# One decoder trunk on one core: the delta rule's recurrence moved into the next head's levels, its projection regrouped

## The reference, cut to what matters

```python
def chunk_gated_delta_rule(q, k, v, g, beta):          # 8 heads, chunks of C tokens
    gc = cumsum(g); decay = exp(gc_i - gc_j) for i >= j, else 0
    a_mat = strict lower part of (k*beta) k^T * decay
    t_mat = inverse of (I + a_mat)                       # triangular solve
    u = t_mat @ (v * beta);  w = t_mat @ (k * beta * exp(gc))
    qk = lower part of q k^T * decay
    for each chunk:                                      # lax.scan: the recurrence
        v_new = u - w @ state
        o     = (q * exp(gc)) @ state + qk @ v_new
        state = state * exp(g_last) + (k * exp(g_last - gc))^T @ v_new

def mixer_c(h, ...):                                     # layer 2 of 4
    qkv, gate, b, a = split(h @ w_in)                    # then a 4-tap causal convolution, silu,
    q, k = l2_norm(q), l2_norm(k)                        # l2 norms, beta = sigmoid(b), g from a
    o = rms_norm(chunk_gated_delta_rule(...), o_gain) * silu(gate)
    return o @ w_out
# around it, for x of 512 tokens x 1024: x += mixer(rms_norm(x)); x += relu(rms_norm(x) @ w1)^2 @ w2
```

## Time and profile before

| | us |
|---|---|
| median of 3 runs (lowest, highest) | 2833.29 (2832.78, 2839.81) |
| the profiled execution | 2835.61 |
| its span, first to last instruction | 2833.8 |
| TensorE busy | 2743.4 (97%) |
| VectorE, ScalarE, GpSimd busy | 1030.9, 1076.0, 1383.0 |

### The profile page before, as it was taken

The page is one execution under the profiler, slowest core; times in us unless marked ns, Lnnn a source line. Parts: engine busy times, 40 slices in busy tenths (PEclk is TensorE's granted clock), DMA queues, the critical chain, the costliest instruction groups (busy, mean ns, idle before and its releaser), DMA issues.

```text
span 2833.8 us, 37226 instructions
## 1 busy us (share of the span) xinstructions
PE 2743.4 (97%) x14594; PEld 2192.7 (77%) x14594; DVE 1030.9 (36%) x1924; ACT 1076.0 (38%) x1625; POOL 1383.0 (49%) x1074
## 2 busy tenths in 40 slices
PE   7999999999989999999999998999999999999999
PEld 5977678888765788887777776888887977688887
DVE  3035431113495522213677774311122044522112
ACT  4355442224346432324334333422233355533221
POOL 3566544444446344455343442444445466544443
PEclk8999999999999999999999999999999999999999
DMA  4232122333422132324211110323322322123232
GB/s 124 90 85 58 45 90 90 104 97 96 102 48 68 53 104 92 101 89 112 60 46 46 46 46 17 103 90 103 102 91 83 109 55 68 45 94 100 89 104 74
DMA packets 271885, 227.82 MB, mean 80 GB/s; under 512 B 29205, under 2 KB 259349, under 8 KB 271749
## 3 DMA queue, kind: packets, MB, share of 16 engines
q1 hardware_dynamic: 260880, 216.29, 25.2%
q10 hardware_dynamic: 10868, 9.66, 1.5%
HBM read 223.62 MB, written 2.30 MB: 80 GB/s over the span
## 4 chain that ended last, share of the span: by engine, by line
PE 88%; DVE 5%; ACT 3%; POOL 1%; issue 1%; DMA 0%; ACTq 0%; DVEq 0%; POOLq 0%
PE bank L1794 49%; PE bank L1703 18%; PE bank L1855 5%; PE bank L2083 2%; PE bank L1830 2%; PE bank L2172 2%; PE bank L1748 1%; PE bank L1908 1%; PE bank L1924 1%; POOL w_lo L561 1%; PE bank L1892 1%; ACT w_hi L707 1%; PE bank L2010 1%; PE bank L1938 1%; PE bank L1885 1%
## 5 line engine op out<-in xcount | busy, mean ns | idle before, releaser
L561 POOL TENSOR_TENSOR w_lo<-raw,w_hi 128x512 fp32r<-128x512 f32 x808 | 1070.5, 1354 | 1193.1 <-ACT w_hi L707 1193.1
L707 ACT ACTIVATE w_hi<-raw 128x2048 fp32r<-128x2048 f32 x202 | 385.6, 1909 | 456.9 <-PE bank L1794 423.3
L1794 PE MATMUL bank<-h_hi,w_hi 128*128 128x512 f32 x1024 | 400.8, 391 | 0.0
L1794 PE MATMUL bank<-h_hi,w_lo 128*128 128x512 f32 x1024 | 398.4, 389 | 0.0
L1794 PE MATMUL bank<-h_lo,w_hi 128*128 128x512 f32 x1024 | 398.4, 389 | 0.0
L1794 PE MATMUL bank<-g_hi,w_hi 128*128 128x512 f32 x1024 | 398.3, 389 | 0.0
L1794 PE MATMUL bank<-g_lo,w_hi 128*128 128x512 f32 x1024 | 398.3, 389 | 0.0
L1794 PE MATMUL bank<-g_hi,w_lo 128*128 128x512 f32 x1024 | 398.3, 389 | 0.0
L1703 PE MATMUL bank<-h_hi,w_hi 128*128 128x512 f32 x776 | 324.1, 418 | 7.2 <-POOL w_lo L561 7.2
L1703 PE MATMUL bank<-h_lo,w_hi 128*128 128x512 f32 x776 | 313.9, 404 | 0.0
L1703 PE MATMUL bank<-h_hi,w_lo 128*128 128x512 f32 x776 | 311.7, 402 | 0.0
(11 more groups left out here) (258 smaller groups left out, 3824.5 us busy)
## 6 DMA issues: line engine op xcount, KB each, us to landing
raw<-in_mlp_w SPq DMA_DIRECT2D x128, 1024.0 KB, 5.2
raw<-in_a_w_in SPq DMA_DIRECT2D x48, 512.0 KB, 5.1
raw<-in_c_w_in SPq DMA_DIRECT2D x32, 512.0 KB, 5.4
raw<-in_a_w_in SPq DMA_DIRECT2D x12, 1024.0 KB, 5.0
raw<-in_b_w_in SPq DMA_DIRECT2D x18, 256.0 KB, 4.0
raw<-in_a_w_out SPq DMA_DIRECT2D x4, 1024.0 KB, 4.9
raw<-in_b_w_in SPq DMA_DIRECT2D x4, 1024.0 KB, 5.5
arena<-bias_scratch ACTq DMA_DIRECT2D x16, 256.0 KB, 3.6
```

What stands on the lines that cost most here:

```text
L561: ins = nc.gpsimd.tensor_tensor(w_lo[s][:, k, :], raw[s][:, k, :], w_hi[s][:, k, :].bitcast(F32), ALU.subtract)
L707: nc.scalar.activation(w_hi[s][:], raw[s][:], ACT.Copy).then_inc(w_hi_done, 1)
L1794: mm = nc.tensor.matmul(lin_bank[j][:], w[s][:, c, P * j:P * j + P], a[:, c, :], start=c + z == 0, stop=c == CT - 1 and z == 2)
```

## The change

The layer's four functions are written in another order; the numbers computed are the same, with the same matmuls.
- **TensorE**: the recurrence and output of head r = h-1 are issued between the products of the levels of head h (`added_values`, `from_state`, `to_state`, `query_sum`, `output_sum`), the last head's on its own at the end. The projection of head h+1 comes as 72 steps in a row behind the gate rows, 6 behind the transposes of `Um`, and 6 each behind W of the levels 1, 2 and 4. Key transposes, value transposes, key products and rows of the next head are spread over the levels 2 to 6. `to_state(r, 0)` has a new wait for the copy of the value tile.
- **VectorE**: the first three tiles' copies, both first convolutions and two silus of head h+1 come before level 1; the state steps of head r come in levels 1 to 3.
- **ScalarE**: three tanh, the rounding of a chunk, the copies of the new values, the output's squares and norm move to other places; the rounding of the first chunk stands ahead of the copy of `Tm`.
- **GpSimd**: that chunk's split stands behind the third mask rather than behind the sixth.
- Tiles used by both heads at a time are double (`Um`, `qe`, `qkd`, `v_beta`, `k_dec`), the gate tile is triple; banks change for three results (`ds_bank`, `wt_bank`, `sum_bank`).

```diff
--- before.py
+++ after.py
@@ tiles and banks
-        qe, grow, decay, qkd, at = (four() for _ in range(5))
+        grow, decay, at = (four() for _ in range(3))
-        Tm, Um, Wm = four(), four(), four()
-        v_beta, k_beta, k_dec, wt = four(), four(), four(), four()
+        Tm, Wm, k_beta, wt = four(), four(), four(), four()
+        Ums, qes, qkds, v_betas, k_decs = ([four(), four()] for _ in range(5))
-        FILL = dict(rows=34, t=38, wt=80, vn=(83, 83, 83, 83), o=83, osum=96)
-        FILL_W = {k: 38 + 7 * k - 4 for k in range(1, LEVELS)}
-        FILL_TW = {k: 38 + 7 * k for k in range(1, LEVELS)}
@@ GpSimd
+                        if k == 3 and h + 1 < C_HEADS:
+                            split_ahead(n0 + 3 + 2 * h)
                     if h + 1 < C_HEADS:
-                        split_ahead(n0 + 3 + 2 * h)
                         split_ahead(n0 + 4 + 2 * h)
@@ ScalarE, per head (r = h - 1; new_values, output_squares, output_norm, high hold the lines moved)
                     act.preload_act_table_set("exp_and_others")
+                    if nxt:
+                        c_tanh(i, [(h + 1, 0)])
+                        round_ahead(n1 + 2 * h + 2)
                     nc.scalar.activation(Tm, bk4(2), ACT.Copy).then_inc(t_init, 1)
+                    if nxt:
+                        c_tanh(i, [(h + 1, 1)])
                     for k in range(1, LEVELS):
                         act.wait_ge(w_done, 6 * h + k)
                         nc.scalar.activation(Wm, bk4(3), ACT.Copy).then_inc(w_copied, 1)
+                        if k <= NB:
+                            new_values(r, k - 1)
                         if k == 3 and nxt:
-                            round_ahead(n1 + 2 * h + 2)
+                            c_tanh(i, [(h + 1, 2)])
+                            key_squares(h + 1)
+                        if k == 4:
+                            if r >= 0:
+                                c_tanh(i, [(r, 3)])
+                                output_squares(r)
+                            act.preload_act_table_set("natural_log_exp_and_others")
                         if k == 5:
-                            query_squares(h)
+                            if r >= 0:
+                                output_norm(r)
+                            if nxt:
+                                key_scales(h + 1)
+                    query_squares(h)
                     act.wait_ge(wt_done, h + 1)
+                    nc.scalar.activation(wt, bk4(wt_bank(h)), ACT.Copy, scale=-1.0).then_inc(wt_copied, 1)
                     if nxt:
                         round_ahead(n1 + 2 * h + 3)
+                    if r >= 0:
+                        high(r)
@@ VectorE, per head
+                    nc.vector.tensor_tensor(qkds[h % 2], bk4(7), decay, ALU.mult).then_inc(qkd_done, 1)
                     if nxt:
                         c_copy(i, h + 1, 0)
+                        conv_steps(i, h + 1, 0, range(4))
+                        c_copy(i, h + 1, 1)
+                    keys_scaled(h)
+                    if nxt:
+                        conv_steps(i, h + 1, 1, range(4))
+                        silu(h + 1, 0)
+                        c_copy(i, h + 1, 2)
+                    nc.vector.tensor_tensor(qes[h % 2], chunks(cy[h % 2][0]), grow, ALU.mult)
+                    if r >= 1:
+                        low(r - 1)
+                    if nxt:
+                        silu(h + 1, 1)
                     for k in range(1, LEVELS):
                         dve.wait_ge(tw_done, 6 * h + k)
 ...                     (the two subtractions of the level, as before)
+                        if k < NB and r >= 0:
+                            state_step(r, k - 1)
+                        if nxt:
+                            if k == 1:
+                                conv_steps(i, h + 1, 2, (0, 1, 2))
+                            if k == 2:
+                                conv_steps(i, h + 1, 2, (3,))
+                            if k == 3:
+                                silu(h + 1, 2)
+                        if k == 4:
+                            if nxt:
+                                c_copy(i, h + 1, 3)
+                            if r >= 0:
+                                silu(r, 3)
+                            if nxt:
+                                key_sums(h + 1)
+                        if k == 5 and nxt:
+                            key_cols(h + 1)
+                    if r >= 0:
+                        output(r)
@@ TensorE, per head (evicted = copy_first[i] + 2 + 4 * (h + 1))
+                    if nxt:
+                        fill(h + 1, 0, 24)
+                    else:
+                        fill(h + 1, 0, 15, (first_out,))
+                    pe.wait_ge(wt_copied, h)
+                    if nxt:
+                        fill(h + 1, 24, 72)
+                    else:
+                        fill(h + 1, 0, 15, (1 - first_out,))
                     pe.wait_ge(u_done, 7 * h + 1)
                     for c in range(NB):
                         mm = nc.tensor.transpose(bk4(2)[:, c, :], Um[:, c, :], ident)
                     mm.then_inc(t_turned, 1)
+                    fill(h + 1, 72 if nxt else 15, 78 if nxt else 18)
                     for k in range(1, LEVELS):
 ...                     (waits and four products into bank 3: w_done)
-                        filler(FILL_W[k])
+                        if r >= 0:
+                            if k == 1:
+                                added_values(r, 0)
+                            if 2 <= k <= NB:
+                                from_state(r, k - 1)
+                            if k == 5:
+                                query_sum(r)
+                                output_sum(r)
+                        if nxt:
+                            if k in (1, 2, 4):
+                                z = {1: 84, 2: 90, 4: 96}[k]
+                                fill(h + 1, z - 6, z)
+                            if k in (2, 3):
+                                turn_keys(h + 1, range(2 * k - 4, 2 * k - 2))
+                            if k == 6:
+                                key_keys(h + 1)
 ...                     (waits for w_copied and u_done, the products of the halves: tw_done)
-                        filler(FILL_TW[k])
+                        if k <= NB and r >= 0:
+                            if k == 1 and nxt:
+                                pe.wait_ge(copied, evicted + 3)
+                            to_state(r, k - 1)
+                        if k == 4 and nxt:
+                            turn_values(h + 1)
+                        if k == 6 and nxt:
+                            beta_rows(h + 1)
 ...                     (four products for wt, then, for a next head:)
+                        key_queries(h + 1)
+                        if r >= 0:
+                            pe.wait_ge(on_done, r + 1)
+                        gate_rows_spread(h + 1)
+                added_values(LAST, 0)
+                pe.wait_ge(on_done, LAST)
+                query_sum(LAST)
+                for c in range(NB):
+                    if c:
+                        from_state(LAST, c)
+                    if c < 3:
+                        fill(C_HEADS, 18 + c, 19 + c)
+                    to_state(LAST, c)
+                output_sum(LAST)
```

More of the change, by code:

```diff
@@ L304, in trunk @@
         cy = [[part(TOK) for _ in range(3)] for _ in range(2)]
-        cg = [part(TOK) for _ in range(2)]
+        cg = [part(TOK) for _ in range(3)]
         cth = [part(TOK) for _ in range(2)]
@@ L1104, in mixer_c @@
[L1104 to L1120, removed]
@@ L1603, in mixer_c @@
                         nc.vector.tensor_tensor(a, a, packed(7, k), ALU.subtract).then_inc(u_done, 1)
[L1604 to L1614, removed]
-                            if nxt:
-                                silu(h + 1, 0)
-                                silu(h + 1, 1)
-                        else:
-                            nc.vector.scalar_tensor_tensor(state, state, e_last[:, c, h:h + 1], src, ALU.mult,
-                                                           ALU.add).then_inc(state_done, 1)
-                            if c == 1 and nxt:
-                                silu(h + 1, 2)
-                            if c == 2:
-                                silu(h, 3)
@@ new lines, in mixer_c @@
+                        if k == 4:
+                            if nxt:
+                                c_copy(i, h + 1, 3)
[7 more added lines that the diff above has]
+                        output(r)
+                low(LAST - 1)
+                for c in range(NB - 1):
+                    state_step(LAST, c)
+                    if c == 0:
+                        silu(LAST, 3)
@@ L1639, in _ @@
+                output(LAST)
+                low(LAST)
             dve.wait_ge(bias_mm, 1)
@@ new lines, in from_state, with to_state @@
+                def from_state(h, c):
+                    pe.wait_ge(wt_copied, h + 1)
```

(21 more changed lines are left out.)

200 lines of the change are left out of this document (104 added, 96 removed).

## The result

The changed kernel takes **2851.74 us** (median of 5 runs, 2849.67 to 2857.23) against 2834.38 for the kernel before in the same runs: a ratio of **1.0068**, 95% interval 1.0055 to 1.0080. That is slower, by 17 us, where 2844.1 was forecast. The profiled execution took 2851.74, its span is 2849.9, 16.1 more than before.

A forecast was written before the change was run, and what follows sets the result against it. TensorE was taken to bound the kernel, 48.13 us a head. Head 0 +10.8, heads to 6 +4.9, last head -8.6 and clock +2.7, last idle +1.0: +10.8 on 2833.29 gives 2844.1 us; 8-in-10 range 2817 to 2858.

The forecast's parts named there:

- the forecast's own 2837 to 2851: Whole kernel, if level 1 is late on VectorE as forecast: 2844 us, uncertain by 7 in all; chance 0.50.
- the walk: Step-by-step count of one steady head of the changed kernel, engine by engine: 49.15 us against 48.13 before.
- T = 29.0 for 29.4: Time in a steady head, counted from the end of its level 6; TensorE was to start level 2 at 29.4 us.
- the walk's 4.9 us of slowing: VectorE's queue before level 1's subtraction: time a head that GpSimd's split was to add, mainly to second convolution and silu.
- the idle in front of TW of level 1: TensorE, steady heads: second tanh delays ScalarE's copy of `Wm`, so TW starts at 25.05 and not at 23.65.
- The price that no row showed whole: VectorE's silu beside GpSimd's split: bounded by 0.68 and 1.74 us, taken as 1.72 for its two SBUF inputs.
- a clock term only for the last head: Last head, until level 1 is through: two idles drop the clock, filler and products at half pace, +2.7 us.
- rival C: Idle around level 1 drops the clock in every head, level 2 at half pace, about 3 us each: 2862; chance 0.12.
- windows 0 to 6: Head 0's level 6 to head 6's: 47.9 us, then five heads of 49.15, against 288.8 before: +4.9 us.
- the last window: End of head 6's level 6 to the last `g_lo`, 63.4 us before: -8.6 us, with +2.7 for the clock.
- The idle before the last `g_lo`: TensorE at the layer's end: a 4.6 us idle expected to cost +1.0 us through the clock, between 0 and 3.
- Rival B: Level 1 is not late, split and second convolution miss each other or slowing is small: 45.15 us a head, 2820; chance 0.25.

## Why the prediction was right, and where it fell short

- **Direction and range**: slower was forecast, +10.8, and came, +16.1 by span and +17 by the medians; 2851.7 lies between 2817 and 2858, but just above the forecast's own 2837 to 2851.
- **The cause held**: level 1 is late on VectorE because of the split, and the wait for `Um` is gone. The one head of the changed kernel in which the clock stayed up took 49.21 us, and with TensorE kept busy in the wait each of the heads 2 to 6 took 49.2; the walk had said 49.15. W of level 2 began at T = 29.0 for 29.4.
- **That 49.15 and 49.21 lie so close is partly luck.** On VectorE several terms of the walk were off, and nearly cancelled: L1601 began 23.2 us after the decays for the 23.4 of the walk. The second convolution was taken as slowed in all three instructions, about 5.0; only two of them met the split, 4.12. `qe` was taken as 1.5 and took 1.1. `low` was taken as 0.7, unslowed; beside the mask of level 4 it took 1.74. The first convolution's L1504, taken as 0.5, took 1.45 beside the masks (the terms given for the first convolution come to D+10.7, not to the D+11.0 that the walk goes on from; it ended at 11.2). `qkd` began 6.2 after the decays for 6.7. So the walk's 4.9 us of slowing were 3.4 by the split and 2.0 by the masks, which it had not counted as slowing anything. On TensorE the idle in front of TW of level 1 was 0.42 for 1.4, that in front of level 6 0.52 for the 0.7 given as a sign.
- **The price that no row showed whole**, silu beside a split, was taken as 1.72 and is 1.77 (0.69 without it). The rule of the Trainium skill, "GPSIMD Engine Reference", section 1 (Specifications), on shared interfaces and instructions with two SBUF inputs: the trace agrees. The slowing as a whole, of which silu is 1.1 of 3.4 us, turned this change's sign: without the split in that place the same order is 0.4% faster than before.
- **The wrong step is the clock in the steady heads.** The forecast's sum had a clock term only for the last head; for the steady heads it stood at nothing, and rival C, which had it, was priced at +18 with a chance of 0.12. In fact the fall came in five of six heads. The walk had put 1.4 us and 2.6 to 4 us of idle around 1.8 of work there, and I set against it one wait of 2.95 us that had kept its clock. That was one row, and of five waits of 2.75, with only 0.42 of idle before them, four did not keep theirs. Nor was C's own mark, about 3 us of idle together, borne out: 0.42 and 2.75 went without a fall in head 3, and 0.41 and 2.14 with one in head 1. C's price was too high: 3 us a head were forecast and 1.6 measured. With 5 x 1.6 = 8 added, windows 0 to 6 would have been +12.9 for the measured +14.0, and the whole 2852; of the 1.1 that are left, 0.7 are head 1, which takes 48.6 with the clock kept up where the walk had 47.9.
- **The ends.** Head 0 was +9.5 for +10.8, and the last window -6.8 for -5.9, with both idles and the low clock where they were put: 1.66 for 2.6, and 2.85 for 2.7, then 0.61. The idle before the last `g_lo` was 4.33 for 4.6; it dropped the clock too, but the net of all that follows was +0.5 for +1.0. These signs and sizes hold; a point too much in one paid for one too little in the other.
- **Rival B** (no late level 1) was forecast at 2820, and the kernel that makes its condition true ran at 2823.0, with a period of 45.86 for 45.15.

What stays open: why the clock stayed up in head 3 with the same 2.75 us of idle as its neighbours. The length of the idle alone does not decide it: with ScalarE's rounding moved, all five heads with an idle of 2.7 fell, and head 1, with 1.2 and 2.1 of idle, did not, where the changed kernel's head 1, with 0.4 and 2.1, did. Which condition makes it fall was not measured.

## What to carry to other kernels

When work is moved on one engine, look at what its semaphores release on the others: here an early tanh and rounding, with the split placed behind the third mask, let GpSimd's split start on top of VectorE's longest queue, and the 3.4 us of slowing lay exactly in front of the instruction TensorE waited for. Count what lies beside masks as well as beside splits. An idle of TensorE can have two prices, its own length and a slow stretch behind it (here 2.75 us, and in most heads 1.6 more); fill it with work that is due anyway, or move what makes it. A regrouping can be sound and still lose by one line's place: the same order with the split put back, and with the last head's blocking steps spread, is 0.6% faster than the kernel before.

## What the runs showed of the hardware

- Beside GpSimd's three masks a VectorE instruction with one tensor input and a scalar (L1504 of the changed kernel, 128 x 512) took 1.45 us; alone it takes 0.48. The prediction counts 0.5 for it. It loses about as much, 0.97 us, as the silu with its two tensor inputs, 1.08.

```profile
1527.63 1.45 DVE L1504 TENSOR_SCALAR arena<-arena,par 128x512 f32<-128x512 f32 x1
```

The masks beside it, on GpSimd:

```profile
1524.12 4.67 POOL L674 TENSOR_TENSOR arena<-arena 128x512 f32<-128x512 f32 x3
```

- GpSimd is slowed too: the split's four instructions took 6.58 us beside the convolution and silu, and 5.04 at 1519.12 of the same trace, where nearly all of VectorE's instructions had one input in PSUM.
- Equal idles of TensorE, 2.75 us in five heads of one execution, were followed by a fall of the granted clock in four and by none in one. Of the six idles of 0.8 to 1.4 us in front of level 2 (with the filler moved there), and of the six of 0.49 (with `low` and silu moved), none was followed by a fall. In the last head idles of 1.66 and 0.69, with only the transposes between them, were followed by a fall in one kernel's trace and by none in another's.
